# Rows of the experts made and stored by GpSimd, a shorter routing, and earlier down weights, in a two-block transformer kernel

## The chip, the cores and the metric

One NeuronCore of a Trainium2 chip runs the whole program. The metric is device time in microseconds (us). TensorE is PE (PEld is its weight load), VectorE DVE, ScalarE ACT, GpSimd POOL, SyncE SP. All data are float32.

## The reference

Two transformer stages run over x of 512 tokens x 1024 and a context of 256 tokens.

- Block 1: `h = h + mix @ w_out`, then `h = h + (silu(hn @ w_gate) * (hn @ w_up)) @ w_down`, with an RMS norm ahead of each.
- Block 2 has two layers. Each ends in a mixture of experts: `hn = rms_norm(x, gain) * (1 + scale) + shift`, where scale and shift are rows computed from a condition. A router takes the best of 4 groups and the best two of its 4 experts, `out = sum of weight_e * (silu(hn @ gate_e) * (hn @ up_e)) @ down_e` over the two, and `x = x + g * out`. Layer 0 routes 768 tokens (6 tiles of 128), layer 1 only 512 (4 tiles).

## The kernel before, in words

The program is a list of stages. At the end of each, PE, DVE, ACT and POOL meet (`meet`, line 3406): none begins the next stage before all four have finished. SP stands outside and feeds weights ahead, held only by semaphores.

**Projection with norm (`Linear`, `TileNorm`).** Output columns go in blocks of 512. The last block runs tile by tile: PE does 16 matmuls (L353), DVE adds the result to the residual in two steps (L3317 from PSUM times a gate, L3319 adding two SBUF tensors), ACT squares and sums (L496), DVE multiplies by the root (L505). Then PE transposes pairs of tiles (L523), and ACT and DVE take them from PSUM with gain and shift (L537, L539) into `HT`, the turned activations. With three pairs, the first is turned inside the last block, ahead of its last tile. With two pairs (block 1 and layer 1) none is. `RowAndTileNorm` does the same after `w_down`, with a second norm of each row.

**Routing stage (`Router`, `Dispatch`).** PE makes logits from `HT` (L2044). DVE then runs a chain of small dependent instructions (L2118 to L2152): group and expert maxima, weights, one-hot choices. Two matmuls count the tokens ahead of each token (L2176, L2177). DVE places every expert's tokens in quarters of 32 rows and builds one-hot matrices (L2238, L2240). PE turns these into a list of tokens and weights with 2n matmuls (L2181), and DVE meanwhile derives which expert each quarter belongs to (L2251 to L2258). Between the two PE runs `keep_awake`: 36 dummy products (L1056; each is two instructions in the profile).

```
keep_awake(pe, k, 3, 36)
pe.wait_ge(k.step_done.sem, self.hot + 2)
```

In the same stage PE turns `HT` back into token rows (L2056), ACT copies these and stores them to DRAM (`moe_rows`), and POOL loads constants (L2029), stores all of `X` (`rows_away<-X`, L2030), waits for it and in layer 1 loads a gate row (L2033).

**Experts stage.** It begins with `keep_awake` of 17 products in layer 0 and 30 in layer 1. POOL gathers rows by token (L2602), the first two at the start. PE then works on 16 tiles of 128 rows in layer 0 and 12 in layer 1, each with two times 64 gate and up matmuls (L2416) and 32 down matmuls (L2432). Gate and up weights have 4 places, down weights 5, 1 MB a load. `ExpertLoads.fill` on SP loads four experts' gate and up (8 loads; the last two wait until PE has read `HT`), and then:

```
self.router.await_rows(sp)
for landed in self.first_gathers:
    sp.wait_ge(landed[0], landed[1] + 16)
for e in range(DOWNS):
    self.load_down(sp, e)
```

## Time and profile before

| What | us |
|---|---|
| runs of the kernel before | 2084.7, 2090.4, 2091.33 (median 2090.4) |
| the profiled execution: its time, its span | 2086.35, 2084.6 |
| PE busy in the span | 1939.7 (93%) |
| DVE, ACT, POOL busy | 1106.0, 654.2, 191.1 |
| DMA moved | 313.88 MB, 151 GB/s over the span |

Busy shares are averages over stages with different limits. PE is the engine that the others feed nearly everywhere, so time can be had only in stretches in which PE is idle, at its lower clock, or busy with work that nobody reads.

### The profile page before, as it was taken

How to read it: one execution, taken by the hardware profiler on the slowest of the kernel's cores; microseconds unless marked ns; L12 is line 12 of the kernel's file. 1: busy time of each engine (PE TensorE's matmuls, PEld its weight loads, DVE VectorE, ACT ScalarE, POOL GpSimd, SP SyncE). 2: the span in 40 equal slices, each digit the busy share in tenths (PEclk: the TensorE clock that was granted, in tenths of full speed). 3: DMA queues.
4: the chain of work that ended last, by engine and by line, in shares of the span. 5: the costliest groups of instructions: out<-in, count | busy, mean ns of one | idle time of the engine just before them, and what ended most of it. 6: DMA issues, size and time to landing. Idle time of an engine off the chain costs nothing. (4 is left out here: it accounts for less than half of the span.)

```text
span 2084.6 us, 28875 instructions
## 1 busy us (share of the span) xinstructions
PE 1939.7 (93%) x10968; PEld 1062.2 (51%) x10968; DVE 1106.0 (53%) x1878; ACT 654.2 (31%) x1294; POOL 191.1 (9%) x214
## 2 busy tenths in 40 slices
PE   7999999999999999899998999799988999988993
PEld 4554874444444444455645764543325678645330
DVE  2001771387787200367754642567756667446773
ACT  2002661100000100242313641356652656333550
POOL 3000110011111000011200000011102000001101
PEclk9999999999999999999999999999999999999996
DMA  8633101476776320410110000689947020048995
GB/s 262 154 81 131 42 12 41 161 245 240 260 247 223 140 81 20 139 41 11 71 41 29 33 22 0 270 318 346 365 180 265 1 82 2 1 155 330 384 406 191
DMA packets 104247, 313.88 MB, mean 151 GB/s; under 512 B 8695, under 2 KB 42647, under 8 KB 85680
## 3 DMA queue, kind: packets, MB, share of 16 engines
q1 hardware_dynamic: 75008, 184.79, 24.8%
q0 software_dynamic: 22448, 103.09, 13.9%
q10 hardware_dynamic: 6656, 24.15, 2.9%
q8 instruction: 90, 1.47, 0.3%
q14 instruction: 45, 0.37, 0.1%
HBM read 281.52 MB, written 35.73 MB: 152 GB/s over the span
## 5 line engine op out<-in xcount | busy, mean ns | idle before, releaser
L2958 PE MATMUL ps<-wide 128*128 128x512 f32 x704 | 306.0, 594 | 2.3 <-issue 1.3
L2958 PEld LDWEIGHTS ps<-wide 128*128 128x128 f32 x704 | 132.4, 190 | 171.8 <-issue 170.6
L2416 PE MATMUL ps<-wide,X 128*32 x448 | 197.5, 594 | 2.1 <-DVE X L2568 2.1
L2416 PE MATMUL ps<-Z,X 128*32 128x512 f32 x1344 | 197.9, 594 | 0.0
L1667 PE MATMUL ps<-wide 128*128 128x512 f32 (+1 forms) x384 | 150.0, 548 | 0.5 <-issue 0.5
L1178 DVE SCALAR_TENSOR_TENSOR Z<-Z,wide 128x2048 f32<-128x2048 f32 x56 | 131.6, 2350 | 2.8
L824 PE MATMUL ps<-T 64*128 64x256 f32 (+1 forms) x888 | 110.0, 378 | 8.7 <-DVE nm L963 6.7
L1417 PE MATMUL ps<-wide 128*128 128x512 f32 x256 | 112.1, 595 | 2.1 <-issue 1.0
L3283 DVE TENSOR_TENSOR X<-ps,X 128x512 f32<-128x512 f32 x16 | 11.1, 692 | 191.4 <-PE ps L328 98.5
L389 ACT ACTIVATE T<-ps 128x512 f32<-128x512 f32 (+2 forms) x139 | 70.8, 537 | 130.6 <-PE ps L1417 109.8
L2432 PE MATMUL ps<-T,gw 128*32 x336 | 104.0, 608 | 8.1 <-ACT X L2489 8.1
L895 ACT ACTIVATE T<-T,nm 128x768 f32<-128x768 f32 (+3 forms) x112 | 86.7, 775 | 76.7 <-DVE nm L963 76.7
L2416 PEld LDWEIGHTS ps<-wide,X 128*32 128x32 f32 x448 | 47.0, 110 | 124.1 <-issue 124.1
L1667 PEld LDWEIGHTS ps<-wide 128*128 128x128 f32 x384 | 72.8, 193 | 69.2 <-issue 65.4
L2974 ACT ACTIVATE Z<-ps 128x512 f32<-128x512 f32 x22 | 13.1, 597 | 293.2 <-PE ps L2958 293.1
L2432 PE MATMUL ps<-wide,gw 128*32 128x512 f32 x224 | 104.0, 608 | 0.0
L2432 PE MATMUL ps<-X,gw 128*32 128x512 f32 x224 | 104.0, 608 | 0.0
L824 PEld LDWEIGHTS ps<-T 64*128 64x128 f32 x888 | 86.3, 192 | 30.2 <-issue 14.0
L391 DVE COPY T<-ps 128x512 f32<-128x512 f32 (+2 forms) x113 | 69.6, 637 | 58.2 <-PE ps L1417 47.8
L870 PE MATMUL ps<-T,Z 128*64 128x128 f32 x1504 | 98.9, 278 | 0.4 <-ACT wide L911 0.4
L353 PE MATMUL ps<-wide 128*128 128x512 f32 x224 | 97.1, 593 | 0.3
L496 ACT ACTIVATE T<-X 128x1024 f32<-128x1024 f32 x24 | 25.3, 1056 | 206.4 <-DVEq L3320 127.0
(394 smaller groups left out, 3363.6 us busy)
## 6 DMA issues: line engine op xcount, KB each, us to landing
wide<-in_experts SPq DMA_DIRECT2D x64, 1024.0 KB, 8.5
Z<-in_mod_w POOLq DMA_DIRECT2D x32, 1024.0 KB, 5.2
T<-in_experts SPq DMA_DIRECT2D x32, 1024.0 KB, 10.9
X<-in_mod_w POOLq DMA_DIRECT2D x16, 1024.0 KB, 5.4
moe_out<-X ACTq DMA_DIRECT2D x28, 512.0 KB, 8.5
wide<-in_w_gate SPq DMA_DIRECT2D x22, 512.0 KB, 5.3
wide<-in_w_up SPq DMA_DIRECT2D x22, 512.0 KB, 6.7
wide<-in_w_in SPq DMA_DIRECT2D x10, 1024.0 KB, 10.2
```

Source lines behind the costliest of these rows:

```text
L353: last = pe.matmul(self.banks.bank(u0 + i)[:, 0:cn], self.lhs(k0 + c, t), w[:, c, :], start=(k0 + c == 0), stop=(k0 + c == self.nk - 1))
L389: return eng.activation(out, src, ACT.Copy, scale=1.0 if scale is None else scale)
L391: return eng.tensor_copy(out, src)
L824: last = pe.matmul(self.S(i, h)[:, at:at + m], q, keys, start=True, stop=True)
L870: last = pe.matmul(k.ps[64 * h:64 * h + 64, 7, t * P:(t + 1) * P], u["values"][b](h), self.PT[:, j % 2, h, b * P:(b + 1) * P], start=(b * ...
L895: last = act.activation(p, p, ACT.Exp, scale=-1.0, bias=k.nm[:, pi % 2, c:c + 1], accum_out=k.den[:, pi % 2, c:c + 1])
L1178: ins = dve.scalar_tensor_tensor(acc, w, by, acc, ALU.mult, ALU.add)
L1417: last = pe.matmul(self.banks.bank(u), w, k.HT[:, c, 0:SEQ], start=(c == 0), stop=(c == DK - 1))
L1667: last = pe.matmul(self.lin.bank(u)[:, 0:cn], k.HT[:, c, t * P:(t + 1) * P], w[:, c % 4, :], start=(c == 0), stop=(c == DK - 1))
L2416: last = pe.matmul(ps[rows, t % 2, :], mo.xT[:, c, rows], w_rows, start=(c == 0), stop=(c == DK - 1))
L2432: last = pe.matmul(ps[rows, 5 + hf, :], mo.hidT[:, c, rows], w_rows, start=(c == 0), stop=(c == 1))
L2958: last = pe.matmul(self.gu.bank(u)[:, 0:self.n], w, self.rhs(c), start=(c == 0), stop=(c == DK - 1))
```

## The change

1. `TileNorm(inside=True)`: every pair but the last is turned inside the last block, and tile i is normed right behind its own residual add instead of behind the next one. `RowAndTileNorm` likewise.
2. `GatedTurned.begin`: PE does the first half of the columns of the first two feed-forward units of block 1 around the turning of the last pair.
3. `RowStores`: during the projection ahead of each routing, POOL loads gain, scale and shift rows and the constants, and for each tile stores `X`, makes the row from the normed tile with two `tensor_tensor` of 128x1024 and stores it. PE's turning back and ACT's copies and stores go.
4. `Router`: logits of all tiles but the last two are made ahead of the last pair's turning. Fewer DVE steps lead to the choice.
5. `Dispatch`: one scan in place of n-1 adds, rounding by a large constant in place of compare-and-count, the token list by matmuls packed four to a row of the array and one transpose. The list of experts now comes behind the token list on DVE, and the first two gathers are issued from this stage.
6. SP no longer waits for the two gathers before the first five down loads.
7. `ModSums` stores all four pieces of two rounds (16 small stores, before 8).

```
n = len(self.blocks) * len(tiles)
         self.banks = Banks(k, owners or alternate(n))
         done = lambda eng, i: self.banks.taken(eng, n - len(tiles) + i)
-        self.norm = norm(done) if callable(norm) else norm and TileNorm(k, norm, done, 0 if n == 8 else 4)
+        self.norm = norm(done) if callable(norm) else norm and TileNorm(k, norm, done, 0 if n == 8 else 4, inside=True)
...
-        self.begun = 0
+        self.begun, self.between, self.after = 0, None, None
...
+            if self.between:
+                self.between(pe, self.norm)
             self.norm.tensor(pe)
+            if self.after:
+                self.after(pe)
...
-            if i == len(self.tiles) - 2 and len(self.norm.pairs) == 3:
-                self.norm.turn(pe, 0)
+            for p in self.norm.behind.get(i, ()):
+                self.norm.turn(pe, p)
         pe.drain().then_inc(k.weights_used, 1)
...
-                    if self.norm and c0 == self.blocks[-1][0] and i:
-                        self.norm.tile(eng, ch, i - 1)
-                        if i == len(self.tiles) - 1 and len(self.norm.pairs) == 3:
-                            self.norm.take(eng, name, 0)
+                    if self.norm and c0 == self.blocks[-1][0]:
+                        self.norm.tile(eng, ch, i)
+                        for p in self.norm.behind.get(i, ()):
+                            self.norm.take(eng, name, p)
                 u += 1
     def vector(self, dve, ch):
         self._take(dve, "dve", ch)
         if self.norm:
-            self.norm.tile(dve, ch, len(self.tiles) - 1)
             self.norm.vector(dve, ch)
...
+        self.behind = {2 * p + 2: [p] for p in range(len(self.pairs) - 1)} if inside else {}
+        self.rest = range(len(self.pairs) - 1 if inside else 0, len(self.pairs))
...
+    def pair_taken(self, pe, p):
+        self.banks.taken(pe, 4 * p + 2)
+        self.banks.taken(pe, 4 * p + 3)
...
+        self.behind, self.pairs = {1: [0], 2: [1]}, self.norm.pairs
...
-        return {1: (0, 1), 2: (2, 3)}.get(i % 3, ())
+        return (0, 1, 2, 3) if i % 3 else ()
...
+class RowStores(Stage):
...
+    def gpsimd(self, pool, ch):
+        k, mo = self.k, self.k.mo
+        for dst, src in self.loads:
+            pool.dma_start(dst, src).then_inc(k.row_mods_landed.sem, 16)
+        for dst, src in ((mo.iota, k.C["iota"]), (mo.token, k.C["token"]), (mo.before, k.C["before"]), (mo.pace, k.C["pace"][:, self.l, :])):
+            pool.dma_start(dst, src).then_inc(k.small_landed.sem, 16)
+        pool.wait_ge(k.row_gains_ready.sem, self.ready + len(self.sets))
+        for i, t in enumerate(self.norm.tiles):
+            gain, shift = self.sets[0 if t < ST else 1]
+            row = self.place(i)
+            pool.wait_ge(k.norm_rows.sem, self.norm.rows + i + 1)
+            pool.dma_start(self.away[:, t, :], k.X[:, t, :]).then_inc(k.spilled.sem, 16)
+            ch.step(pool.tensor_tensor(row, self.norm.hn[:, t, :], gain, ALU.mult))
+            ch.wait()
+            ch.step(pool.tensor_tensor(row, row, shift, ALU.add))
+            ch.wait()
+            pool.dma_start(self.rows_out[t * P:(t + 1) * P, :], row).then_inc(k.rows_stored.sem, 16)
+    def vector(self, dve, ch):
+        k = self.k
+        dve.wait_ge(k.row_mods_landed.sem, self.landed + 16 * len(self.loads))
+        for gain, _ in self.sets:
+            dve.scalar_tensor_tensor(gain, gain, 1.0, self.gain, ALU.add, ALU.mult).then_inc(k.row_gains_ready.sem, 1)
...
+        self.lots = [(0, len(tiles) - 2), (len(tiles) - 2, len(tiles))]
+        self.banks = Banks(k, ["act", "dve", "dve"], 0 if len(tiles) == NT else 4, 4)
...
+        self.stores.await_consts(pool)
+        self.stores.await_spilled(pool)
         for dst, src in self.rows_gate:
             pool.dma_start(dst, src).then_inc(k.small_landed.sem, 16)
-        pool.wait_ge(k.small_landed.sem, self.consts + 64 + 16 * len(self.rows_gate))
+        self.stores.await_rows(pool)
...
+    def first_logits(self, pe, norm):
+        for p in range(len(self.tiles) // 2 - 1):
+            norm.pair_taken(pe, p)
+        self.logits(pe, 0)
...
-        for v in range(2 * len(self.tiles)):
-            t, hf = self.tiles[v // 2], v % 2
-            self.rows.may_fill(pe, v)
-            for c in range(4):
-                last = pe.transpose(self.rows.bank(v)[:, c * P:(c + 1) * P],
-                                    k.HT[:, 4 * hf + c, t * P:(t + 1) * P], k.ident[:, :])
-            self.rows.filled(last)
...
+        do(dve.tensor_reduce(m, k.rL[:, 0:n, 0:4], AXX, ALU.max))
+        do(dve.tensor_tensor(G, k.rL[:, 0:n, 0:4], over4(m), ALU.subtract))
         dve.drain().then_inc(k.step_done.sem, 1)
...
+        do(dve.scalar_tensor_tensor(O, G, 0.0, ordered, ALU.is_equal, ALU.mult))
+        first_of(O)
...
         dve.wait_ge(k.step_done.sem, self.e + 2)
         dve.drain().then_inc(k.step_done.sem, 1)
...
+        do(dve.scalar_tensor_tensor(a, E, 0.0, ordered, ALU.is_equal, ALU.mult))
+        do(dve.tensor_reduce(k.rs[:, 3, 0:n], b, AXX, ALU.add))
+        first_of(a)
+        wa, wb = mo.weight[:, 0, 0:n], mo.weight[:, 1, 0:n]
         dve.wait_ge(k.step_done.sem, self.e + 4)
...
-        first_max(E, a, wa)
-        do(dve.scalar_tensor_tensor(k.rG[:, 0:n, :], a, -2.0, E, ALU.mult, ALU.add))
-        first_max(k.rG[:, 0:n, :], b, wb)
-        do(dve.tensor_tensor(m, wa, wb, ALU.add))
-        do(dve.reciprocal(m, m))
-        do(dve.tensor_tensor(m, m, k.rs[:, 3, 0:n], ALU.mult))
-        dve.tensor_tensor(wa, wa, m, ALU.mult)
-        dve.tensor_tensor(wb, wb, m, ALU.mult)
+        do(dve.scalar_tensor_tensor(G, a, -2.0, G, ALU.mult, ALU.add))
+        do(dve.tensor_reduce(wb, G, AXX, ALU.max))
+        do(dve.tensor_tensor(b, G, over4(wb), ALU.is_equal))
+        do(dve.tensor_tensor(b, b, ordered, ALU.mult))
+        first_of(b)
+        do(dve.tensor_tensor(E, a, b, ALU.add))
...
+        do(dve.tensor_tensor(mo.either[:, 0:NEXP * n].rearrange("p (g j n) -> p n g j", g=4, n=n), spread(E), groups, ALU.mult))
+        dve.drain().then_inc(k.step_done.sem, 1)
...
+        do(dve.scalar_tensor_tensor(m, wb, 1.0, k.rs[:, 3, 0:n], ALU.add, ALU.mult))
+        do(dve.reciprocal(wa, m))
+        do(dve.tensor_tensor(wb, wb, wa, ALU.mult))
...
+        self.banks.filled(pe.matmul(self.banks.bank(0)[:, 0:16 * n], mo.ones, both, start=True, stop=True))
+        self.banks.filled(pe.matmul(self.banks.bank(1)[:, 0:16 * n], mo.before, both, start=True, stop=True))
+        keep_awake(pe, k, 7, 36)
         pe.wait_ge(k.step_done.sem, self.hot + 2)
         for u in range(2 * n):
-            last = pe.matmul(self.banks.bank(2)[:, 0:2 * self.m], mo.row_hot[:, u, :], mo.quad_hot[:, u, 0:2 * self.m],
-                             start=(u == 0), stop=(u == 2 * n - 1))
+            j = u % 4
+            last = pe.matmul(self.banks.bank(2)[32 * j:32 * j + 32, 0:P], mo.quad_hot[:, u, :], mo.row_hot[:, u, :],
+                             start=(u < 4), stop=(u >= 2 * n - 4))
         self.banks.filled(last)
+        self.banks.taken(pe, 2)
+        self.banks.filled(pe.transpose(self.banks.bank(3)[:, 0:P], mo.listed, k.ident[:, :]))
+    def gpsimd(self, pool, ch):
+        pool.wait_ge(self.k.tokens_ready.sem, self.tokens + 1)
+        self.gathers(pool)
...
+        size = NEXP * n
+        self.banks.await_full(dve, 0)
+        self.banks.take(0, dve.tensor_tensor_scan(mo.sums[:, 1:size + 1], mo.joined[:, 0:size], self.banks.bank(0)[:, 0:size],
+                                                  0.0, ALU.mult, ALU.add))
+        self.banks.taken(dve, 0)
...
+        do(dve.tensor_scalar(mo.quarters, count, QUARTER / 2 - 0.5, ROUND * QUARTER, ALU.add, ALU.add))
+        ch.step(dve.memset(preceding[:, :, 0], 0.0))
+        do(dve.tensor_scalar(mo.quarters, mo.quarters, ROUND * QUARTER, float(QUARTER), ALU.subtract, ALU.max))
         do(dve.tensor_tensor_scan(mo.end, mo.ones[:, 0:NEXP], mo.quarters, 0.0, ALU.mult, ALU.add))
-        do(dve.tensor_scalar(mo.spare, mo.end[:, NEXP - 1:NEXP], -1.0, float(4 * m), ALU.mult, ALU.add))
+        do(dve.tensor_scalar(mo.spare, mo.end[:, NEXP - 1:NEXP], -1.0, float(P * m), ALU.mult, ALU.add))
...
-        do(dve.scalar_tensor_tensor(rank, over_tokens(mo.first), float(QUARTER), rank, ALU.mult, ALU.add))
-        for i in range(2):
-            do(dve.tensor_tensor(tmp, mo.chosen[:, i, 0:n, :], rank, ALU.mult))
-            do(dve.tensor_reduce(at[:, n * i:n * i + n], tmp, AXX, ALU.add))
+        self.banks.await_full(dve, 1)
+        self.banks.take(1, dve.tensor_tensor(rank, self.banks.bank(1)[:, 0:size].rearrange("p (e n) -> p n e", n=n),
+                                             preceding.rearrange("p e n -> p n e"), ALU.add))
+        self.banks.taken(dve, 1)
+        do(dve.tensor_tensor(rank, rank, mo.first.unsqueeze(1).to_broadcast((P, n, NEXP)), ALU.add))
+        do(dve.tensor_tensor(tmp, mo.chosen[:, :, 0:n, :], rank.unsqueeze(1).to_broadcast((P, 2, n, NEXP)), ALU.mult))
+        do(dve.tensor_reduce(at.rearrange("p (a n) -> p a n", a=2), tmp, AXX, ALU.add))
+        do(dve.tensor_scalar(at_quad, at, 0.5 - P / 2, ROUND * P, ALU.add, ALU.add))
+        do(dve.tensor_scalar(at_quad, at_quad, ROUND * P, None, ALU.subtract))
+        do(dve.tensor_tensor(at_row, at, at_quad, ALU.subtract))
+        ch.step(dve.tensor_tensor(mo.row_hot[:, 0:2 * n, :], mo.iota.unsqueeze(1).to_broadcast((P, 2 * n, P)),
+                                  at_row.unsqueeze(2).to_broadcast((P, 2 * n, P)), ALU.is_equal))
+        quads = mo.quad_hot[:, 0:2 * n, 0:m]
+        do(dve.tensor_tensor(quads, mo.iota_quad[:, 0:m].unsqueeze(1).to_broadcast((P, 2 * n, m)),
+                             at_quad.unsqueeze(2).to_broadcast((P, 2 * n, m)), ALU.is_equal))
...
+        dve.drain().then_inc(k.step_done.sem, 1)
         dve.tensor_copy(k.token_rows[:, :, 0:n], at.rearrange("p (a n) -> p a n", a=2))
-        do(dve.tensor_scalar(at_row, at, 1.0 / P, None, ALU.mult))
-        count_of(at_quad, at_row, 2 * n, m - 1, ALU.is_ge)
-        do(dve.scalar_tensor_tensor(at_row, at_quad, -float(P), at, ALU.mult, ALU.add))
...
+        self.banks.await_full(dve, 2)
+        self.banks.take(2, dve.tensor_copy(mo.listed, self.banks.bank(2)[:, 0:P]))
+        self.banks.await_full(dve, 3)
+        parts = self.banks.bank(3)[:, 0:P].rearrange("p (j c) -> p c j", j=4)
+        self.banks.take(3, dve.tensor_reduce(k.row_pair[:, :], parts, AXX, ALU.add))
+        self.banks.taken(dve, 3)
+        dve.tensor_copy(k.row_token[:, 0:m], k.row_pair[:, 0:m]).then_inc(k.tokens_ready.sem, 1)
+        do(dve.tensor_scalar(mo.end, mo.end, 1.0 / QUARTER, None, ALU.mult))
...
-        self.router.await_rows(sp)
-        for landed in self.first_gathers:
-            sp.wait_ge(landed[0], landed[1] + 16)
+        self.router.stores.await_rows(sp)
         for e in range(DOWNS):
             self.load_down(sp, e)
...
+    def begin(self, pe, u, norm=None):
+        if norm:
+            norm.pair_taken(pe, 0)
+        for s in self.slots[0]:
+            self.k.rg.await_landed(pe, s)
+        self.unit(pe, u, slice(0, self.n // 2))
+        self.begun.add(u)
...
+        projection.early.then.between = lambda pe, norm: feed.begin(pe, 0, norm)
+        projection.early.then.after = lambda pe: feed.begin(pe, 1)
+        add(feed)
...
+            projection.between = router.first_logits
...
+            dispatch.gathers = experts.first_gathers
...
```

## Rows read from the trace of the kernel before

**Rows 1.** Stage windows: PE, PEld, DVE, ACT, POOL busy (x), PEclk, DMA share, GB/s.
```profile
1318.66:1328.76 10.10, 5.35 (x33) 5.14 (x33) 8.69 (x18) 5.42 (x11) 0.00 (x0) 0.83 0.89 357
1328.76:1358.18 29.42, 21.69 (x186) 17.97 (x186) 20.70 (x84) 10.21 (x19) 2.97 (x5) 0.98 0.96 382
...
1367.01:1560.26 193.25, 188.02 (x1688) 64.79 (x1688) 138.89 (x156) 114.49 (x109) 21.37 (x14) 0.99 0.82 314
...
1854.20:1863.61 9.41, 5.22 (x32) 4.78 (x33) 7.01 (x14) 5.31 (x11) 0.00 (x0) 0.82 0.89 351
1863.61:1891.73 28.12, 19.90 (x144) 17.38 (x144) 17.14 (x81) 8.03 (x15) 3.43 (x6) 0.83 0.91 355
...
1902.67:2053.95 151.28, 142.49 (x1264) 48.50 (x1264) 107.38 (x116) 78.58 (x70) 13.66 (x10) 0.99 0.85 348
```
**Rows 2.** Chain that ended last: start us, us, what.
```profile
1863.86 2.12 POOL Z L2029 x4
1865.98 20.98 DMA rows_away<-X
```
**Rows 3.** Timeline of layer 0's routing: start us, us, engine, line, instruction.
```profile
1332.57 0.66 DVE L2109 TENSOR_REDUCE rL<-ps 128x120 f32<-128x480 f32 x1 [0.53 <-PE ps L2050]
1333.58 0.18 DVE L2118 TENSOR_REDUCE rs<-rL 128x6 f32<-128x24 f32 x1
...
1340.92 0.07 DVE L2207 MEMSET Z<- 128x16 f32 x1 [0.17 <-DVE Z L2205]
...
1343.29 8.23 PE L1056 MATMUL ps<-ident 128*128 128x128 f32 x72
...
1351.07 1.75 DVE L2240 TENSOR_TENSOR Z<-Z 128x1536 f32<-128x1536 f32 x1
...
1353.58 2.87 PE L2181 MATMUL ps<-Z 128*128 128x32 f32 x24 [2.05 <-DVEq L2248]
```
**Rows 4.** Timeline of layer 1's routing.
```profile
1863.61 1.92 PE L2044 MATMUL ps<-wide,rw 128*32 128x512 f32 x16 [1.15 <-ACTq L3406]
...
1875.58 9.89 PE L1056 MATMUL ps<-ident 128*128 128x128 f32 x72
```
**Rows 5.** Windows, columns as in rows 1.
```profile
1340.00:1345.00 5.00, 4.40 (x36) 3.81 (x37) 1.98 (x13) 3.60 (x7) 0.00 (x0) 1.00 1.02 420
1858.00:1862.00 4.00, 2.79 (x14) 2.82 (x15) 2.96 (x7) 1.80 (x5) 0.00 (x0) 0.57 1.02 426
1892.00:1896.00 4.00, 4.00 (x20) 4.00 (x21) 2.23 (x2) 1.91 (x1) 3.18 (x2) 0.50 0.43 126
```
**Rows 6.** Timeline at the end of layer 1's projection.
```profile
1847.33 0.69 DVE L3317 TENSOR_TENSOR T<-ps,Z 128x512 f32<-128x512 f32 x1 [4.36 <-PE ps L353]
...
1854.20 0.69 DVE L3317 TENSOR_TENSOR T<-ps,Z 128x512 f32<-128x512 f32 x1 [4.36 <-PE ps L353]
...
1857.40 0.75 DVE L505 TENSOR_SCALAR T<-X,rstd 128x1024 f32<-128x1024 f32 x1
...
1859.21 3.26 PE L523 MATMUL ps<-ident,T 128*128 128x128 f32 x16 [2.98 <-DVE wide L539]
```
**Rows 7.** Timeline of the linear attention, where POOL and DVE both compute.
```profile
957.69 3.44 POOL L1985 TENSOR_TENSOR T<-T 128x1536 f32<-128x1536 f32 x1 [22.73 <-ACT T L1823]
959.16 3.59 DVE L1904 TENSOR_TENSOR T<-T 128x1536 f32<-128x1536 f32 x1
```
**Rows 8.** Timeline at the ends of block 1's two projections.
```profile
377.42 0.69 DVE L3283 TENSOR_TENSOR X<-ps,X 128x512 f32<-128x512 f32 x1 [5.32 <-PE ps L353]
377.49 1.96 PE L523 MATMUL ps<-ident,T 128*128 128x128 f32 x16
...
384.44 7.99 PE L2958 MATMUL ps<-wide 128*128 128x512 f32 x18 [0.96 <-ACTq L3406]
...
860.46 0.69 DVE L3283 TENSOR_TENSOR X<-ps,X 128x512 f32<-128x512 f32 x1 [17.69 <-PE ps L353]
...
876.29 2.79 PE L1629 MATMUL ps<-wide 128*32 128x512 f32 x32 [1.15 <-ACTq L3406]
```

More of the change, by code:

```diff
@@ L468, with __init__ @@
 class TileNorm(Stage):
-    def __init__(self, k, sets, ready, first, hn=None):
+    def __init__(self, k, sets, ready, first, hn=None, inside=False):
         super().__init__(k)
@@ L486, in scalar @@
         for i in range(len(self.tiles)):
-            if i == len(self.tiles) - 1 and len(self.pairs) == 3:
-                self.take(act, "act", 0)
             self.square(act, i)
-        for p in range(len(self.pairs) == 3, len(self.pairs)):
+            for p in self.behind.get(i, ()):
+                self.take(act, "act", p)
+        for p in self.rest:
             self.take(act, "act", p)
@@ L641, in vector @@
     def vector(self, dve, ch):
-        self.norm.tile(dve, ch, ST + 1)
         self.norm.vector(dve, ch)
```

261 lines of the change are left out of this document (125 added, 136 removed).

## The prediction

> **What bounds the kernel now.** I cut the span into stages with the view of windows. In the two expert stages PE is busy 188.02 of 193.25 us and 142.49 of 151.28 us at full clock; around them lie stretches that PE does not fill: the ends of the projections (10.10 and 9.41 us), the routing stages (29.42 and 28.12 us) and the starts of the experts, from the end of one window to the start of the next (8.83 and 10.94 us) [rows 1]. Next the chain of waits, read only where it leaves PE. Layer 1's routing hangs on POOL: 2.12 us of constants, then the store of X, 20.98 us, because the stage cannot end before it [rows 2]. Layer 0's is not in that chain, so there I read the timeline: DVE's chain of small steps sets it, from the sum of the logits at 1332.57 to the one-hots at 1353.58, and then the list of experts to 1358.18 [rows 1, 3]. Below, S is the start of a routing stage, X its end, E the end of the last projection matmul.
>
> The clock matters in these stretches. It stood at 0.57 in the window after PE had waited 2.98 us, and 16 transposes took 3.26 us instead of the 1.96 us they take in block 1 [rows 5, 6, 8]; at the start of layer 1's experts it was 0.50, which is the 1.2 GHz level [rows 5]. The same 72 dummy matmuls took 8.23 us in layer 0, where PE had been turning rows back until just before, and 9.89 us in layer 1 [rows 3, 4].
>
> **Block 1.** After w_out PE needed 7.02 us from 377.42 to the first feed-forward matmul at 384.44 [rows 8]. Afterwards one pair is turned inside (+1.95). The last tile is normed 3.3 us after its matmuls, its pair turned by 5.25, and the second half-unit done by 7.0; two half-units, eight matmuls each at half of the 0.43 us spacing, 3.5 us, are then ahead: 1.95 + 7.0 - 3.5 = 5.5, a gain of 1.5. Half-width matmuls load weights twice, so I take 1.3 (bounds 0 and 1.6). After w_down the way was 15.83 us [rows 8]. Now: 1.95 inside, 6.45 to the last norm (residual add 0.7, then two rounds of square and root 1.6 with a DVE step of 1.45 and one of 0.95), 3.26 for cold transposes [rows 6], 1.4 to take them and meet: 13.1. I take a gain of 2.5 (bounds 1.5 and 3.9, the latter with warm transposes). Sum: -3.8.
>
> **Ends of the two later projections.** Before, 10.10 and 9.41 us from E to S [rows 1]. One pair moves inside in each (+1.95). The last norm was done 3.95 us after E (1854.20 to 1858.15) [rows 6]. PE fills part of the wait with logits, 1.9 us in layer 0 and 1 us in layer 1, the rest is idle.
>
> What is new here is POOL computing beside DVE. A DVE tensor_tensor that began at 959.16 beside a POOL one ended at 962.75, 1.62 us after POOL's end at 961.13: it waited that operation out and then ran its own length. By element count a row takes POOL 2 x 2.29 us [rows 7], plus two DMA issues of 0.53 [rows 2], 5.7 us against 6.87 from tile to tile [rows 6], so POOL keeps up. But row i-1 is still in work when tile i's residual add (L3319, two SBUF inputs) comes: put on one time line, the add waits about 1.2 us. So the last norm lands at E + 5.2, PE has then been idle over 3 us and turns cold (3.26), and takes and meeting add 1.2: S = E + 9.65, 11.6 with the pair inside. That is +1.5 in layer 0 and +2.2 in layer 1; with neither lock nor cold clock it would be 9.1 (-1.0 and -0.3), with the add and the norm each waiting out a whole POOL operation 15 (+5 each). Sum: +3.7.
>
> The loads of gain and shift rows (5 x 512 KB and 3 x 512 KB more) come at the projection's start, well ahead of DVE's first residual add; I cost them at nothing, and if they were late DVE would catch up over PSUM's eight banks. The eight more small stores of block 1 are issued by an idle ACT and land before the stage's end: nothing.
>
> **Routing stage, layer 0.** First the logits: half are ready, but ACT's table load and copy lead to a sum at S + 3.35, before S + 3.81 [rows 1, 3]. From there to the one-hot of both choices were 8.35 us; now there are 18 small steps at 0.215 (0.18 busy [rows 3] and the wait) and five larger ones, 6.15: S + 9.5. DVE then needs 1.1 for weights and, for the placing, 7.0: a scan (0.3), fifteen small steps (3.4), two of 192 elements (0.8), the row one-hot of 1.75 [rows 3] and three quad one-hots; its one-hots stand at S + 17.6, where they stood at S + 24.8.
>
> But PE does not get there. It has 0.9 us of counting matmuls, then the unchanged 36 dummy products. With the turning back of rows gone, PE has been idle 6 us, twice the wait that dropped the clock before, so I take 10.3 us for them (bounds 8.23 [rows 3] and 15.3, all at 0.213 as at the lower clock): S + 20.7, three us behind DVE. Then 24 packed matmuls. Each is a quarter as wide as the logits', of which 16 took 1.92 us [rows 4], so 24 would be 0.7; unpacked 24 took 2.87 [rows 3]. I take 1.1, near the packed row, which has the same form. Copy, transpose, sum and cast of the list: 1.2. The list of experts used to run beside PE, 4.6 us from one-hots to X [rows 1, 3]; now it follows. X = S + 20.7 + 1.1 + 1.2 + 4.6 = S + 27.6: -1.8 (bounds -4, and +3 with slow dummies).
>
> The Trainium skill, page TensorEngine Tiling (Array Packing), section Tiling Modes, has tiles of the array work in parallel; by it alone the 24 matmuls are six groups, about 0.7 us, and the sum would be 0.4 lower in this layer.
>
> **Routing stage, layer 1.** The same with four tiles. Sum of logits at S + 2.7, choice at S + 8.3, DVE's one-hots at S + 15.6, PE's dummies done at S + 8.3 + 0.9 + 10.3 = S + 19.5, then 0.8 + 1.2 + 3.8: X = S + 25.3 against 28.12: -2.8 (bounds -6.5 and 0). The store of X, 20.98 us here [rows 2], starts tile by tile during the projection and its last 512 KB leave at about E + 6; with 8 MB of expert weights at 420 GB/s [rows 5] in front of and beside it, it lands by E + 20, the last row by E + 22, and tokens exist at about E + 31. So POOL no longer sets the end. Should they come later than that, each us counts.
>
> **Start of the experts.** The two gathers leave 4.6 us before X. The five down loads, 5.2 MB, 12.5 us at that rate, now follow the gate and up loads at about E + 22 and run until E + 36, so a gather lands under full traffic, which I give 11 us. PE is busy with dummies until X + 6.6 and X + 9, which covers it. The way from X to the first matmul stays 8.83 and 10.94: 0 (if the gathers were late, up to +2).
>
> **Expert stage, layer 1.** Layer 0 gives 188.02/16 = 11.75 us a tile; four tiles fewer would be 146.25, and layer 1 took 151.28 [rows 1]. The excess of 5 us stands after a stretch in which the DMA engines were busy only 0.43 of the time [rows 5], and at full traffic they are the limit. With 5.2 MB moved into that hole and 3 MB of rows and stores into the projection, the queue runs 12 us ahead. I take -4 (bounds -5 and 0).
>
> **Sum.** -3.8 + 3.7 - 1.8 - 2.8 + 0 - 4.0 = -8.7 on the profiled execution's 2086.35: 2077.7. That execution lies 4 us under the median shown, and the runs scatter by 6.6, so a median of new runs lies between 2077.7 and 2081.7; I take 2080.
>
> **Rivals.**
> - *PE stays warm.* The logits in the wait and half-filled stretches keep the clock up: transposes 1.3 less twice, dummies 8.23 twice: -6.8, 2073. For it: layer 0's 0.98 clock in routing [rows 1], though held there by work that goes. Against it: 0.57 after less idle time.
> - *The lock paces the projection.* If both DVE operations with shared ports wait out POOL operations of 2.29 us, a tile's chain is 3.95 + 4.6 = 8.5 us. It decides from 6.87 on: beyond, every tile slips, 1.7 us x 5 and x 3 tiles, 13.6 us, less the 2.5 already counted: 2091, slower. For it: the full wait in rows 7. Against it: L3317 reads PSUM, and a step of POOL's fits between the two. The Trainium skill, page GPSIMD Engine Reference, section Engine selection, sends elementwise work on tiles to VectorE and expects GpSimd to be about twice as slow with two inputs; the trace agrees as far as it goes (3.44 against 1.62 us).
> - *The early down loads give nothing*, since places and not traffic hold the late loads back: the -4 goes, 2084. The same if the gathers come late.
> - *The change does not do what it says*: rows land after the tokens, since they queue behind 8 MB; every stage end waits again on a store, 2086.
>
> **Chances.** Forecast 0.50, warm 0.15, no gain from the loads 0.18, rows late 0.07, lock 0.10. A difference below 0.3%, 6.3 us, is what a measurement cannot tell from none. Faster holds warm, most of the forecast and some of the third: 0.62; same 0.28; slower 0.10. Range 2069 to 2088, which leaves the lock and part of warm outside.
>
> **What would show it.** Right: dummies of routing over 9.5 us with the clock at 0.5 to 0.8 and PE's list matmuls waiting on PE, not DVE; L3319 over 1 us long on late tiles; routing stages of 27 to 28 and 25 us; layer 1's experts near 147 us. Wrong: a clock of 1.00 through routing, a store or row landing after the token list, gathers landing after the dummies, or POOL's last row later than the next residual add in every tile.

## The result: slower by 1.2%

| Kernel | runs | median us | range us | ratio to the kernel before, 95% |
|---|---|---|---|---|
| before | 4 | 2088.7 | 2084.7 to 2091.3 | |
| changed | 4 | 2115.5 | 2113.0 to 2116.9 | 1.0123 [1.0108, 1.0138] |

The profiled execution of the changed kernel took 2116.89 us (span 2115.1), that of before 2086.35. So 30.5 us have to be found. First the view of windows of the changed kernel, cut at the same events as [rows 1]: end of the last projection matmul E, start of the routing stage S, its end X, first expert matmul, end of the last; first layer 0, then layer 1 (columns: window, its length, busy time and count of each engine, granted PE clock, DMA share, GB/s).

```profile
1317.54:1337.99 20.45, 5.28 (x32) 3.61 (x32) 5.22 (x8) 4.79 (x9) 8.22 (x6) 0.69 0.95 378
1337.99:1368.58 30.59, 15.62 (x123) 13.40 (x124) 18.75 (x75) 2.42 (x6) 2.32 (x2) 0.67 0.70 280
1368.58:1376.73 8.15, 7.10 (x42) 6.87 (x43) 3.37 (x4) 3.10 (x4) 0.29 (x1) 0.72 0.00 0
1376.73:1569.96 193.23, 188.02 (x1688) 64.77 (x1688) 138.83 (x156) 114.53 (x109) 21.58 (x14) 0.99 0.77 286
1866.70:1887.89 21.19, 4.50 (x32) 3.69 (x33) 5.41 (x8) 4.79 (x9) 8.44 (x6) 0.69 0.93 371
1887.89:1917.42 29.53, 15.35 (x113) 12.80 (x113) 16.35 (x75) 2.18 (x6) 2.67 (x3) 0.67 0.78 303
1917.42:1928.81 11.39, 10.34 (x68) 10.11 (x69) 3.37 (x4) 3.10 (x4) 0.28 (x1) 0.77 0.01 1
1928.81:2084.50 155.69, 144.31 (x1264) 48.67 (x1264) 107.56 (x116) 79.02 (x70) 14.90 (x10) 0.97 0.77 308
```

Against [rows 1]: the ends of the projections grew from 10.10 and 9.41 us to 20.45 and 21.19 (+22.1), the routing stages from 29.42 and 28.12 to 30.59 and 29.53 (+2.6), the starts of the experts changed by -0.7 and +0.5, layer 0's experts not at all, layer 1's by +4.4. Between the two layers 2.8 us were added (1569.96 to 1866.70, against 1560.26 to 1854.20). What lies ahead of layer 0's E gave 1.1 back. Sum +30.6.

Now the chain of waits, from layer 0's E on (start, length, engine and line; "POOLq" is the time until POOL's sequencer had done its part of the meeting, line 3500):

```profile
1323.29 2.38 POOL Z L2051
1325.74 2.34 POOL Z L2053
1328.07 0.27 issue
1328.34 9.61 POOLq L3500
1337.99 1.94 PE ps L2112 x16
...
1348.86 9.95 PE ps L1065 x72
...
1361.76 1.35 POOL X L2666
1363.11 5.42 POOLq L3500
1368.58 6.23 PE ps L1065 x34
```

In layer 1 the same two pieces are 10.12 and 5.44 us. POOL had made its last row at 1328.08 and issued its store at 1328.37; nothing is left for it to do, and yet the meeting hangs on it until 1337.95. The view of DMA, cut to that issue, gives 8.6 us from issue to landing (columns: transfer, queue, kind, count, size, us). Below it is the same view's line on POOL's queue, q0, from 1328.9 to 1337.0 (packets, MB, share of the 16 engines):

```profile
moe_rows<-Z POOLq DMA_DIRECT2D x1, 512.0 KB, 8.6
q0 software_dynamic: 246, 0.88, 26.7%
```

From 1337.0 to 1341.0 that queue moves nothing. The 0.88 MB are more than the last row: the store of the last tile of `X`, issued at 1322.73, was still in the same queue.

1328.37 + 8.6 = 1336.97, one us ahead of the next stage; in layer 1 1877.75 + 9.4 = 1887.15 for a stage that starts at 1887.89; the second gather, issued at 1363.42, landed 5.0 us later, at 1368.4, and the experts' stage began at 1368.58. `meet` makes each engine drain (an instruction that waits for the engine's own earlier work) before it counts as arrived. From here on the theory is called landing: POOL's drain waits until the transfers that POOL itself issued have landed.

### The profile page after: what moved, and what is told of

Its sections match the earlier page's. It is cut to its first block, busy times and chain, and to the rows that moved or that the text cites. A ratio compares the mean times of both kernels' runs of the same rounds, so it can differ in the third digit from the quotient of the medians.

```text
span 2115.1 us, 28841 instructions
## 1 busy us (share of the span) xinstructions
PE 1934.1 (91%) x10938; PEld 1060.7 (50%) x10938; DVE 1115.7 (53%) x1866; ACT 644.0 (30%) x1274; POOL 251.6 (12%) x260
## 4 chain that ended last, share of the span: by engine, by line
PE 73%; issue 8%; DVE 5%; PEld 4%; DMA 4%; POOLq 2%; PEldq 1%; POOL 1%; ACT 1%; SPq 0%; DVEq 0%; ACTq 0%
PE ps L3021 14%; PE ps L358 7%; PE ps L2481 7%; PE ps L1676 6%; PE ps L329 6%; PE ps L833 5%; PE ps L879 4%; PE ps L854 4%; PE ps L2822 4%; PE ps L2497 3%; PE ps L1652 2%; PE ps L1065 2%; POOLq L3500 2%; PEld ps L1426 2%; PE ps L1426 1%
## 5 line engine op out<-in xcount | busy, mean ns | idle before, releaser
L3021 PE MATMUL ps<-wide 128*128 128x512 f32 (+1 forms) x736 | 306.5, 575 | 1.9 <-issue 1.7
L3021 PEld LDWEIGHTS ps<-wide 128*128 128x128 f32 x736 | 138.3, 190 | 166.2 <-issue 164.1
L1676 PE MATMUL ps<-wide 128*128 128x512 f32 (+1 forms) x384 | 150.0, 548 | 0.5 <-issue 0.5
L1426 PE MATMUL ps<-wide 128*128 128x512 f32 x256 | 113.8, 603 | 2.1 <-issue 1.0
L1676 PEld LDWEIGHTS ps<-wide 128*128 128x128 f32 x384 | 72.8, 193 | 69.2 <-issue 65.3
L395 DVE COPY T<-ps 128x512 f32<-128x512 f32 (+2 forms) x113 | 69.7, 637 | 58.1 <-PE ps L1426 47.8
L358 PE MATMUL ps<-wide 128*128 128x512 f32 x224 | 97.6, 593 | 0.3
L502 ACT ACTIVATE T<-X 128x1024 f32<-128x1024 f32 x24 | 25.3, 1056 | 213.3 <-DVEq L3409 128.9
## 6 DMA issues: line engine op xcount, KB each, us to landing
wide<-in_w_in SPq DMA_DIRECT2D x10, 1024.0 KB, 10.5
```

Of the source, the lines that this page charges most:

```text
L358: last = pe.matmul(self.banks.bank(u0 + i)[:, 0:cn], self.lhs(k0 + c, t), w[:, c, :], start=(k0 + c == 0), stop=(k0 + c == self.nk - 1))
L1426: last = pe.matmul(self.banks.bank(u), w, k.HT[:, c, 0:SEQ], start=(c == 0), stop=(c == DK - 1))
L1676: last = pe.matmul(self.lin.bank(u)[:, 0:cn], k.HT[:, c, t * P:(t + 1) * P], w[:, c % 4, :], start=(c == 0), stop=(c == DK - 1))
L3021: last = pe.matmul(self.gu.bank(u)[:, columns], w, self.rhs(c)[:, columns], start=(c == 0), stop=(c == DK - 1))
```

## Experiments

Each was timed against the kernel before on the same chip, but they ran on several chips; where two experiments are compared, the ratios to the kernel before (with their 95% intervals) carry the comparison. In the kernel before the last three columns read 10.1, 9.4; 48.4, 48.5; 193.2, 151.3 [rows 1].

| Kernel | median us | ratio, 95% | E to S | E to first expert matmul | experts, layers 0, 1 |
|---|---|---|---|---|---|
| changed | 2115.5 | 1.0123 [1.0108, 1.0138] | 20.5, 21.2 | 59.2, 62.1 | 193.2, 155.7 |
| met_rows | 2104.1 | 1.0070 [1.0053, 1.0087] | 11.7, 11.8 | 52.2, 55.8 | 193.4, 154.8 |
| met_both | 2087.0 | 0.9990 [0.9980, 1.0001] | 11.7, 11.8 | 47.6, 47.8 | 195.1, 155.0 |
| gathers_after_met | 2088.5 | 0.9996 [0.9982, 1.0010] | 11.7, 11.8 | 45.9, 48.6 | 195.0, 152.2 |
| loads_after_rows | 2112.7 | 1.0113 [1.0096, 1.0130] | 14.9, 14.7 | 61.1, 61.2 | 193.4, 154.9 |
| last_on_act | 2100.9 | 1.0059 [1.0038, 1.0081] | 11.7, 12.8 | 51.1, 55.2 | 195.0, 152.5 |
| downs_wait | 2114.7 | 1.0123 [1.0106, 1.0140] | 20.8, 21.3 | 59.4, 62.2 | 194.8, 152.2 |
| before_downs | 2098.8 | 1.0041 [1.0025, 1.0057] | 11.4, 9.3 | 54.0, 48.9 | 195.7, 152.8 |
| both_downs | 2090.0 | 0.9998 [0.9987, 1.0009] | 11.6, 11.8 | 45.9, 48.2 | 194.6, 152.2 |
| both_downs_22 | 2087.1 | 0.9984 [0.9971, 0.9997] | 11.7, 11.8 | 44.8, 46.2 | 196.5, 155.5 |
| thin | 2079.1 | 0.9953 [0.9938, 0.9967] | 7.2, 8.8 | 41.8, 44.6 | 194.4, 155.1 |
| met_first | 2084.7 | 0.9972 [0.9957, 0.9987] | 9.5, 10.0 | 45.5, 47.3 | 195.1, 152.3 |
| met_first_22 | 2077.1 | 0.9942 [0.9920, 0.9964] | 9.4, 10.0 | 40.8, 44.0 | 194.3, 154.9 |
| best_again | 2080.7 | 0.9954 [0.9940, 0.9968] | 9.5, 9.6 | 42.3, 41.8 | 195.2, 155.0 |
| best_downs | 2081.8 | 0.9953 [0.9937, 0.9969] | 9.5, 9.3 | 42.2, 43.0 | 195.2, 155.2 |

The stage lengths are those of one profiled execution each. The time at which E is reached in layer 0 lies between 1314.0 and 1321.6 us in them, so the stages tell more than a difference of two spans.

**met_rows**

```
+        pool.memset(k.pool_flag[:, :], 0.0).then_inc(k.stage_done, 1)      # behind the last row's store
...
 def meet(eng, i):
-    eng.drain().then_inc(k.stage_done, 1)
+    if not (eng is pools[0] and getattr(stages[i], "pool_met", False)):
+        eng.drain().then_inc(k.stage_done, 1)
```

> The changed kernel, but GpSimd does not drain at the meeting that ends the two projections with row making: after issuing the last row's store it writes one column (memset of 128x1) and that instruction counts as its arrival. Theory (landing): the drain waits until the last store has landed (issued 1328.37 and 1877.75, stage starts 9.6 and 10.1 us later), while GpSimd's instructions don't. Then the memset runs at once, ends of projections shrink from 20.4 and 21.2 us to 11 to 12 us, and the time falls by 17 to 20 us to about 2097. Rival (descriptors): GpSimd itself is held for those 10 us by making the transfer's descriptors; then the memset starts 9 us late and the time stays at 2115. Rival (given back): stages start earlier, but the expert loads or the later meeting take it back: the gain stays under 8 us.

The timeline of this run:

```profile
1329.21 0.59 POOL L2057 DMA_DIRECT2D moe_rows<-Z  x1 [0.30 <-POOL Z L2055]
1329.79 0.12 POOL L2058 MEMSET pool_flag<- 128x1 f32 x1
1329.96 1.94 PE L2115 MATMUL ps<-wide,rw 128*32 128x256 f32 x16 [3.30 <-POOL pool_flag L2058]
...
1354.67 0.97 POOL L2669 DMA_INDIRECT X<-moe_rows,row_token  x1 [0.30 <-issue]
1362.18 6.41 PE L1066 MATMUL ps<-ident 128*128 128x128 f32 x34 [10.59 <-POOLq L3504]
```

The memset ran at once, so POOL was never held by making descriptors: that rival falls. The ends shrank by 8.8 and 9.4 us as expected, but the time by 11.3 only, not 17 to 20. Part was given back at the next meeting, where POOL still drains: the gathers were now issued 8.7 us earlier, beside the expert loads, landed after 6.8 and 6.4 us instead of 5.3 and 5.0, and PE waited 10.6 us.

**met_both**

```
         self.gathers(pool)
+        pool.memset(self.k.pool_flag[:, :], 0.0).then_inc(self.k.stage_done, 1)
```

> As the run before, and GpSimd meets in the same way after the first two gathers, which it issues inside the routing stage. Theory (landing): the routing stages end when the expert lists stand, at 1365.1 and 1913.6 in the changed kernel and not at 1368.6 and 1917.4, so 3.4 and 3.8 us more are gained: about 2090 in all. Rival: the first matmul of the experts hangs on the gathered rows or on PE's dummies and not on the meeting, and nothing more is gained than without the drain at the projections (2097).

The time came out 17 us under met_rows and 3 under the 2090 expected; 13 of the 17 are seen from E to the first expert matmul (4.7 and 8.0). The windows of both layers, E to S, S to X, X to the first matmul:

```profile
1313.98:1325.63 11.65, 3.90 (x33) 2.23 (x32) 5.18 (x8) 4.67 (x9) 8.40 (x7) 0.93 0.92 342
1325.63:1353.25 27.62, 15.95 (x124) 13.73 (x124) 18.74 (x75) 2.42 (x6) 2.43 (x3) 0.69 1.01 415
1353.25:1361.54 8.29, 7.21 (x42) 6.97 (x43) 3.41 (x4) 3.13 (x4) 0.33 (x1) 0.71 0.25 100
...
1852.60:1864.42 11.82, 4.75 (x33) 3.77 (x33) 5.42 (x8) 4.79 (x9) 8.57 (x7) 0.66 0.90 343
1864.42:1889.36 24.94, 14.46 (x113) 11.91 (x113) 16.36 (x75) 2.18 (x6) 2.79 (x4) 0.71 1.02 425
1889.36:1900.41 11.05, 10.01 (x68) 9.77 (x69) 3.37 (x4) 3.10 (x4) 0.28 (x1) 0.79 0.48 196
```

**gathers_after_met**: as met_rows, with `self.first_gathers(pool)` moved from the routing stage to the start of `Experts.gpsimd`.

> The kernel that meets without a drain only at the ends of the projections (2104), with the first two gathers issued after the routing stage's meeting, as in the kernel before. GpSimd drains there, but its last transfers have landed by then. Theory (landing): the meeting no longer waits for the gathers, which cost 10.6 us from PE's last work to the next stage there; the gathers now land after it, and the first expert matmul comes 9 to 11 us after the meeting instead of 8.3 to 9.8: time about 2088 to 2091, so the early gathers with their draining meeting cost 13 us or more and without it bring 1 to 3 us. Rival (the meeting was late for another reason): the time stays at 2100 or more.

The time came as expected; from X to the first matmul it took 7.8 and 11.3 us, where 9 to 11 had been expected. The early gathers brought nothing that a measurement tells (2087.0 beside 2088.5; the intervals overlap), and with their draining meeting they cost 15.6 us (2104.1 against 2088.5).

**loads_after_rows**

```
         sp.wait_ge(k.weights_used, self.n0)
+        self.router.stores.await_rows(sp)
         for e in range(PLACES):
```

> The changed kernel, but SP issues none of the 8 MB of gate and up weights before all rows have landed (they were issued at the end of the projection, ahead of and beside the last stores). The drain stays. Theory (landing): the last store lands faster without that traffic, in 3 to 5 us after its issue and not 8.6 to 9.4, so the ends of the projections shrink by 4 to 6 us each, 8 to 12 us in all; the weights (20 us at 420 GB/s) still land before the first expert matmul, which comes 39 us after the meeting: about 2105. Rival (descriptors, or a fixed cost of the drain): the wait stays 9 to 10 us and the time at 2115.

The timeline, and the DMA view of the last store alone:

```profile
1325.05 0.59 POOL L2055 DMA_DIRECT2D moe_rows<-Z  x1 [0.30 <-POOL Z L2053]
1328.09 5.25 SPq L2390 DMA_DIRECT2D wide<-in_experts  x8
1329.05 1.93 PE L2112 MATMUL ps<-wide,rw 128*32 128x256 f32 x16 [7.91 <-POOLq L3500]
```

```profile
moe_rows<-Z POOLq DMA_DIRECT2D x1, 512.0 KB, 3.0
```

The wait follows the traffic: landed at 1328.05, stage at 1329.05, again one us apart; a fixed cost is out. The ends gave 12.0 us, but the time fell by 2.8 us, not by the 10 expected. The delayed weights met the gathers: the second was issued at 1354.88 and the meeting hung on it until 1366.80, so that from S to the first matmul it took 46.2 and 46.5 us instead of 38.7 and 40.9.

**last_on_act**

```
+class LastRow(Stage):                     # last part of the stage
...
+    def scalar(self, act, ch):
...
+        act.wait_ge(k.norm_rows.sem, s.norm.rows + i + 1)
+        act.dma_start(s.away[:, t, :], k.X[:, t, :]).then_inc(k.last_spilled.sem, 16)
+        act.wait_ge(k.last_row_made.sem, self.made + 1)
+        act.dma_start(s.rows_out[t * P:(t + 1) * P, :], s.place(i)).then_inc(k.last_stored.sem, 16)
```

> The changed kernel with all its draining meetings, but ScalarE, which has nothing else left to do there, issues the last tile's two stores (the spill of X and the row that GpSimd has made); GpSimd's last own transfer is then the row before it. Theory (landing, and only of transfers that go through GpSimd's queue): GpSimd's drain ends when the row before has landed, about 12 us after the projection's last matmul, ScalarE's drain does not wait for its stores, and the ends of the projections shrink from 20.5 and 21.2 us to about 12: the time falls like that of the kernel that meets without a drain there (2104, part of it lost again at the gathers), to 2100 to 2106. Rival (any engine's drain waits for the transfers that it issued): ScalarE takes GpSimd's place, the ends stay at 19 to 21 us and the time at 2115.

```profile
1317.48 0.57 POOL L2060 DMA_DIRECT2D moe_rows<-Z  x1 [0.30 <-POOL Z L2058]
...
1325.16 0.35 ACTq L2092 DMA_DIRECT2D moe_rows<-Z  x1
...
1326.99 1.93 PE L2133 MATMUL ps<-wide,rw 128*32 128x256 f32 x16 [4.70 <-POOLq L3523]
```

This separates the engines. POOL's own last store landed after 8.6 us, at 1326.04, and the stage began 0.9 us later, while ACT's store, issued at 1325.16, needed 9.7 us, to 1334.8, and held nobody. A drain on ACT doesn't wait for what ACT issued; on POOL it does. The time, 2100.9 us, lies where the theory put it (2100 to 2106).

The theory holds wherever POOL drained with a transfer of its own in flight at these meetings: 18 in the five runs changed, met_rows, loads_after_rows, downs_wait and last_on_act. The next stage began 0.2 to 1.1 us after POOL's last landing in each, while the time from issue to landing went from 2.9 to 11.8 us. Landing is shown: by taking the drain away, by changing the traffic and by changing the queue.

**downs_wait, before_downs, both_downs, best_downs**: the wait of the first five down loads for the two gathers, put back into three kernels and taken out of the one before.

```
         self.router.stores.await_rows(sp)
+        for landed in self.first_gathers:
+            sp.wait_ge(landed[0], landed[1] + 16)
         for e in range(DOWNS):
```

> The changed kernel, but the first five down loads wait again until the two gathers have landed, as in the kernel before. Theory (places): loading them early only moves the hole in the traffic, since the next gate and up loads wait for a place; layer 1's expert stage goes back from 155.7 us to about 151.5 and the time falls by 2 to 4 us; layer 0's stays at 193. Rival (the early loads do help, and the longer stage comes from the later start of everything): the time rises by 2 to 5 us. Rival (no effect): within 1 us, with the same 4.4 us wait for a down load in layer 1.

> The kernel before with one edit: the first five down loads no longer wait for the two gathers (they still wait for the rows and for the places), so they land during the routing stage. Theory (places): the hole in the traffic moves behind them and closes only when the next gate and up loads get a place; layer 1's expert stage grows from 151.3 to 154 to 156 us and the time by 1 to 4 us, to 2090 to 2093. Rival, my forecast: layer 1's stage falls to 147 and the time to 2085. Second rival: no effect, 151 and 2089.

> The kernel that meets without a drain on GpSimd at both places (2087), and the first five down loads wait for the two gathers again. Theory (places): in the changed kernel this one edit took layer 1's expert stage from 155.7 to 152.2 us; here too it gives 2 to 3.5 us in layer 1, and layer 0 gives 0 to 1.5 us back: about 2085. Rival (noise, or early loads help where the routing is short): 2087 or more, with layer 1's stage at 155.

> The same kernel, but the first five down loads wait for the two gathers, as in the kernel before. Theory (places): holding them back costs nothing, since the next loads wait for a place and not for the queue; the two kernels agree within 2 us, and the 4 us that I forecast from the early loads are not there. Rival, my forecast: without the early loads layer 1's stage grows and the time rises by 3 us or more. Second rival (they do harm, as in the kernel before, where they alone cost 7.5 us): the time falls by 2 to 4 us.

Three of the four kernels show no difference in time: 2114.7 beside 2115.5 (2 to 4 us less were expected), 2090.0 beside 2087.0 on another chip (ratios 0.9998 and 0.9990, intervals overlapping; 2085 was expected), and on one chip 2081.8 beside 2080.7. In the kernel before, the edit alone costs 7.5 us, where 1 to 4 were expected. Its timeline shows where the largest part is lost:

```profile
1361.59 2.60 SPq L2326 DMA_DIRECT2D T<-in_experts  x5
...
1363.06 1.04 POOL L2600 DMA_INDIRECT X<-moe_rows,row_token  x1 [26.87 <-DVEq L3404]
1364.41 0.97 POOL L2600 DMA_INDIRECT X<-moe_rows,row_token  x1 [0.30 <-issue]
...
1372.62 1.97 PE L2406 MATMUL ps<-ident,X 128*128 128x128 f32 x8 [2.89 <-DMA X<-moe_rows,row_token]
```

The five loads start just ahead of the gathers, the gathered rows come late, and X to the first matmul takes 12.8 us instead of 8.83. In the changed kernel the loads leave at 1342.33, well ahead of the gathers at 1361.76, so they do no harm there. Why they do no good is in the next section. Layer 1's expert stage came out near 152 or near 155 us whichever way the loads went; the theory that the early loads lengthen it, which downs_wait seemed to bear out, fell with best_downs. The windows of that stage show what goes with the length, here in both_downs and in met_both:

```profile
1902.32:2054.52 152.20, 141.99 (x1264) 48.54 (x1264) 107.38 (x116) 78.77 (x70) 15.37 (x10) 0.99 0.83 333
1900.41:2055.39 154.98, 144.53 (x1264) 48.93 (x1264) 107.35 (x116) 79.08 (x70) 15.36 (x10) 0.97 0.77 309
```

PE is busy 142.0 or 144.5 us with the same 1264 matmuls, and the granted clock of the stage is 0.99 or 0.97. In the kernel before and the six experiments near 152 us the clock is 0.98 or 0.99 and PE is busy 141.8 to 142.7 us; in the nine kernels near 155, the changed one among them, it is 0.97 or 0.98 and PE is busy 143.6 to 144.9. The lower level lies in two places. Seven of the nine have a dip of 3.4 us some 110 us into the stage (0.51 from 2038.70 to 2042.20 in the changed kernel), behind a wait of PE for DVE of 2.9 us there. And in the last tile the clock is low for 6.8 us in all nine (0.50 from 2076.30 to 2083.10), for 3.4 us in most of the others. The rest of the difference is waits of PE. What brings on the one or the other stays open; met_first_22 waited 2.9 us for DVE too, and has no dip.

**thin**

```
- ch.step(pool.tensor_tensor(row, row, shift, ALU.add))
+ ch.step(pool.tensor_tensor(row[:, 0:8], row[:, 0:8], shift[:, 0:8], ALU.add))    # the multiply likewise
```

> The kernel that meets without a drain at both places, but GpSimd's two operations on a row work on 8 of its 1024 columns (the stored rows are otherwise left as they are in memory, so the experts compute on other values; tokens and lists are the same). Theory: GpSimd's arrival comes 4.5 us earlier, DVE's residual add of the last tile falls from 1.64 us to 0.7, PE's transposes of the last tile start 1 us earlier: the ends shrink from 11.7 to about 8 us in both layers, 6 to 8 us in all: 2080. Rival (the lock costs nothing and something else sets the end): within 2 us of 2087.

POOL computes only 8 of a row's 1024 columns here and leaves out the rest, so the experts get other values. DVE's add of the last tile in met_both and in thin:

```profile
1314.75 1.66 DVE L3414 TENSOR_TENSOR X<-X,T 128x512 f32<-128x512 f32 x1
```

```profile
1315.12 0.69 DVE L3414 TENSOR_TENSOR X<-X,T 128x512 f32<-128x512 f32 x1
```

POOL's row making costs 8 us of time, as expected. 4.4 and 3.0 us of it are at the ends of the projections: the lock on the add (DVE held up while a POOL operation runs) is 1 us each, the rest there is the wait for the last row.

**met_first, met_first_22, best_again**: POOL arrives at the meeting ahead of its last row, which it makes and stores beside the routing stage; then 22 dummy products.

```
+            if i == self.n - 1:
+                pool.memset(k.pool_flag[:, :], 0.0).then_inc(k.stage_done, 1)
             pool.wait_ge(k.norm_rows.sem, self.norm.rows + i + 1)
...
-        keep_awake(pe, k, 7, 36)
+        keep_awake(pe, k, 7, 22)
```

> The kernel that meets without a drain on GpSimd at both places (2087), with GpSimd's arrival at the end of the two projections moved ahead of the last tile's row: it arrives once the row before is made and makes and stores the last one beside the routing stage. There PE waited 4.7 and 3.8 us for GpSimd's arrival. Theory (the last row sets the end, a term that my forecast lacked): the ends of the projections shrink from 11.65 and 11.8 us to 8.5 to 9.5, and 4 to 6 us are gained, less up to 1 us that the routing's first DVE steps wait for GpSimd's operations: about 2082. Rival (ScalarE and VectorE taking the last pair end as late): under 2 us gained.

> As the run before, and 22 dummy products instead of 36 between the counting and the list matmuls of the routing stage. The 72 matmuls of the 36 take 10.2 us there at the low clock, and the one-hots stand 3.2 us (layer 0) and 4.3 us (layer 1) before PE is done with them. Theory (PE's dummies bind the routing stage): 22 take 6.2 us, the one-hots become what is waited for, and 3 and 4 us are gained: 2078. Rival (PE gets colder for it, or the gathers bind the start of the experts): less than 2 us gained.

> As the run before, with 22 dummy products in the routing stage instead of 36. Where the down loads waited for the gathers, the same edit gave 3 us (2090 to 2087). Theory: the same 3 us here, about 2079, faster than the kernel before by 0.4 to 0.5%. Rival: the expert stages, whose loads are planned by places, give part of it back (2081 to 2083).

> The fastest kernel so far once more (GpSimd meets without a drain at both places, arrives ahead of its last row, 22 dummy products), beside its twin with the down loads held back. Expected as measured before: 2077 us, layer 0's expert stage 194 to 195 us, layer 1's 152 to 155.

The earlier arrival gave 2.1 and 1.8 us at the ends (4 to 6 in time were expected, 2.2 came). The fewer dummies gave 3 us with the waiting down loads, where 2078 had been expected and 2087.1 came: from S to X 2.2 and 2.3 us were gained, but the experts took longer (196.5 and 155.5 us for 194.6 and 152.2). Here they gave 4 to 8 (2077.1 and, in the repeat, 2080.7; 2079 and 2077 were expected). The windows of met_first_22:

```profile
1314.33:1323.69 9.36, 5.13 (x33) 3.31 (x33) 5.24 (x8) 3.48 (x7) 6.56 (x6) 0.82 0.88 319
1323.69:1355.16 31.47, 17.19 (x138) 15.30 (x138) 22.45 (x79) 6.83 (x10) 4.57 (x6) 0.78 1.01 420
...
1845.19:1855.20 10.01, 4.75 (x34) 3.78 (x33) 5.43 (x8) 3.48 (x7) 7.22 (x6) 0.69 0.89 332
1855.20:1889.21 34.01, 22.48 (x154) 19.70 (x154) 19.73 (x79) 6.59 (x10) 4.44 (x7) 0.69 0.95 396
```

Here the second and the last row reach from S to the first expert matmul, 31.5 and 34.0 us against 36.0 and 37.3 in met_first. Of the kernels that compute the right values this version and its twin best_downs are the fastest: it is 0.5 to 0.6% ahead of the kernel before in two sets of runs, 1.6 to 1.8% ahead of the change as it was made.

## Why the prediction was wrong

The forecast was 2080 in a range of 2069 to 2088, and slower had a chance of 0.10.

**The step that failed** is "So POOL no longer sets the end", and with it "takes and meeting add 1.2" in the sum for the ends of the projections, where POOL's part of the meeting was put at nothing. The prediction followed the rows as data and found them landed before the tokens, which they were (1337 against 1361). It never asked what POOL must do to leave a stage. The drain at the meeting turned each transfer in flight into a wait of all four engines: 9.6 and 10.1 us for the last store, 3.5 and 3.8 us for the gathers (from the last step of the lists, 1365.1 and 1913.5, to X). That is 27 us, and taking the drains away gave 28.5.

The trace of before did show it, off the critical path, and the prediction read none of it. Timeline of POOL, the drain's own line (its duration in ns, and its start), and the second load's time to landing:

```profile
1244.25 1.08 POOL L2000 DMA_DIRECT2D T<-mod_rows  x2 [103.19 <-PEq L3406]
L3406 POOLq DRAIN  x1: 5477/5477/5477, 1244.7 to 1244.7; - x1
T<-mod_rows POOLq DMA_DIRECT2D x1, 512.0 KB, 5.2
```

The second load, issued at 1244.80, landed at 1250.02, and the drain ended at 1250.14. It cost nothing there, since PE was busy with a projection until 1318. Four more drains of before end 0.4 to 1.6 us after such a landing (at 76.1, 1524.9, 2022.2 and 2079.2 us). At its two routing meetings POOL had waited for its stores and loads by semaphore before it drained, so there nothing was in flight.

The nearest rival had every stage end waiting on a store again, but as data that the gathers need, at 2086 and with a chance of 0.07. The change puts POOL's transfers in flight at the ends of two kinds of stage, and that should have been priced as an added wait with everything behind it.

**E to S**, forecast 11.6 with the pair inside, that is 9.65 behind E. Without the drain it was 11.65 and 11.82, 2 us more each, since the last row (made 10.5 and 10.7 us behind E) and its store come before POOL arrives; this term was missing too. The cold transposes counted for nothing beside it: they took 3.35 us in the changed kernel and 1.97 in met_both's layer 0, where the stage began 11.65 us behind E even so. The lock was right in kind: the add took 1.64 us and 1.82 us beside POOL, 0.69 alone, so 1.0 and 1.1 us where 1.2 was forecast. The rival in which the lock paces the projection did not happen: from 1241 to 1318, the whole projection of layer 0, PE's waits add up to 0.6 us.

**Routing**, forecast S + 27.6 and S + 25.3. met_both has 27.62 and 24.94. The dummies ran cold in 9.95 and 10.19 us (10.3 forecast), clock 0.67, and PE was what the list waited for; the 24 packed matmuls took 0.86 us (1.1 forecast). This chain was right, step by step, and the rival of a warm PE wrong here.

**Start of the experts**, forecast 8.83 and 10.94: 8.29 and 11.05 in met_both.

**Block 1**, forecast -3.8. Two timelines of the changed kernel, at the ends of its two projections:

```profile
379.13 3.69 PE L3021 MATMUL ps<-wide 128*128 128x256 f32 x16 [0.37 <-issue]
```

```profile
865.50 3.68 PE L533 MATMUL ps<-ident,Z 128*128 128x128 f32 x16 [6.37 <-DVE Z L511]
870.32 4.99 PE L1638 MATMUL ps<-wide 128*32 128x512 f32 x32 [1.15 <-ACTq L3500]
875.61 4.96 PE L1652 MATMUL ps<-wide 128*128 128x512 f32 x11 [0.30 <-issue]
```

The stage starts at 870.32 where it started at 876.29 [rows 8], 6 us early, but its first 32 matmuls ran cold (4.99 us where they took 2.79), and the next group starts 3.8 us earlier than before (879.37). The sum was right by luck: two terms were wrong and cancelled. The change at `w_out` gave 3.0 us (`w_down`'s first matmul at 703.92, before at 706.97), not 1.3 with a bound of 1.6, since a half-unit is 16 matmuls of half width and not eight, so that 7 us of work are ahead and not 3.5. The change at `w_down` gave the other 2.9 us (2.5 forecast, cold transposes of 3.68 us included), and the 2.2 us that the cold matmuls behind it cost were in no term.

**Expert stage of layer 1**, forecast -4, measured +4.4. The step that failed is "the queue runs 12 us ahead". SP in the changed kernel:

```profile
1342.33 2.62 SPq L2394 DMA_DIRECT2D T<-in_experts  x5
1383.86 11.32 SPq L2390 DMA_DIRECT2D wide<-in_experts  x4
```

With the five downs gone ahead, nothing is issued for 39 us (40 in layer 1): the next load needs a place, and that comes free when the first tile's gate and up are done, 7.1 us behind the first expert matmul, before as after (1909.80 behind 1902.67, 1935.94 behind 1928.81). The DMA share from X to the first matmul is 0.00 and 0.01 in the changed kernel, 0.37 in layer 0 of before (from 1358.18 to 1367.01). So the hole was moved, not filled; this is the third rival, which had 0.18. It takes the -4 away, but it forecast no loss. Of the +4.4, PE's busy time for the same 1264 matmuls is 1.8 (142.49 to 144.31, at a clock of 0.99 and 0.97), the rest is waits of PE. The kernel best_downs has nearly the same length, 155.2, with the loads waiting.

**What is left without the drains.** The profiled execution of met_both took 2087.63 us, 9.9 over the 2077.7 of the sum: 4.2 from the last row, 7.7 from layer 1's experts, 1.8 from layer 0's (195.07, forecast unchanged), less 2.8 ahead of layer 0's E and 1.0 in smaller terms.

## What to carry to other kernels

Before a transfer is moved to GpSimd in a kernel whose engines drain at a barrier, list what it has in flight there: the barrier waits for the landing, under whatever traffic the other queues make. Let GpSimd arrive by an instruction of its own, or issue the last transfers from ScalarE, whose drain didn't wait. And an earlier load didn't help here, since the one after it could not start earlier. When a sum comes out right, check its terms: block 1's were wrong by 1.7 and 2.2 us.
